# The first key projection moved into the norm of a two-block network kernel, beside the gates and the first query

## The reference

```python
def first_block(x, c, ada_w, ada_b, norm_g, gdn_w_in, ...):
    cond = jax.nn.silu(c)
    mod = cond @ ada_w[i] + ada_b[i]
    shift, scale, gate = jnp.split(mod, 3, axis=-1)
    hdn = rms_norm(x, norm_g[i]) * (1.0 + scale) + shift
    y = gated_deltanet(hdn, ...)
...
def gated_deltanet(h, w_in, conv_w, a_log, dt_bias, norm_w, w_out):
    proj = h @ w_in
    qkv, z, b_lin, a_lin = jnp.split(proj, ...)
    qkv = jax.nn.silu(causal_depthwise_conv(qkv, conv_w))
    q = l2norm(q) * (dh ** -0.5);  k = l2norm(k)
    beta = jax.nn.sigmoid(b_lin)
    g = -jnp.exp(a_log) * jax.nn.softplus(a_lin + dt_bias)
    gc = jnp.cumsum(g, axis=-1)                     # within a chunk
    decay = jnp.exp(gc[..., :, None] - gc[..., None, :])
    ...                                             # chunk by chunk, with a state per head
    return (rms_norm(o, norm_w) * silu(z)) @ w_out
```

## Time and profile before

| | |
|---|---|
| median of 3 runs | 2103.11 us (2101.9 to 2104.24) |
| the profiled execution | 2103.15 us, its span in the trace 2101.4 us |
| PE, DVE, ACT, POOL busy | 95%, 61%, 41%, 7% of the span |
| granted TensorE clock, mean | 0.985 |
| the norm, 30 to 70 us | PE busy 30.30, DVE 36.04 of 40 us, clock 0.79 |
| 150 to 200 us | PE busy 45.45 of 50 us |

### The profile page before, as it was taken

One profiled execution on the slowest core, in us unless ns is written; L12 is line 12 of the kernel. 1 busy time (PEld: TensorE's weight loads), 2 busy tenths in 40 slices (PEclk: granted clock), 3 DMA queues, 4 the chain that ended last, 5 costly groups with the idle time before them and its releaser, 6 DMA issues.

```text
span 2101.4 us, 29428 instructions
## 1 busy us (share of the span) xinstructions
PE 1992.7 (95%) x11256; PEld 1618.2 (77%) x11256; DVE 1272.9 (61%) x2415; ACT 853.5 (41%) x1376; POOL 138.4 (7%) x114
## 2 busy tenths in 40 slices
PE   4989999999999999969998999999999899999998
PEld 2667878888887878857776787777777678888877
DVE  6777777797869686749635644445353435633543
ACT  5644353544345443159403333544443337600321
POOL 0030202021111212000000000000000000000000
PEclk8999999999999999989999999999999999999999
DMA  7222233232323242548213211120312125211232
GB/s 282 86 75 70 87 89 106 65 101 71 105 68 105 67 120 68 168 158 287 80 41 136 66 60 41 41 101 21 111 41 81 61 72 219 91 49 41 85 116 80
DMA packets 128971, 200.27 MB, mean 95 GB/s; under 512 B 56596, under 2 KB 88084, under 8 KB 127808
## 3 DMA queue, kind: packets, MB, share of 16 engines
q1 hardware_dynamic: 128832, 198.39, 29.6%
HBM read 156.22 MB, written 42.11 MB: 94 GB/s over the span
## 4 chain that ended last, share of the span: by engine, by line
PE 47%; DVE 4%; DMA 2%; issue 2%; ACT 1%; SPq 0%; DVEq 0%; ACTq 0%
PE m_job L1682 6%; PE m_job L1684 6%; PE m_job L1683 6%; PE e_b L2369 4%; PE e_b L2371 4%; PE e_b L2370 4%; PE p_out L1352 2%; PE p_out L1353 2%; PE p_out L1354 2%; PE p_sc L1928 2%; PE p_s L1951 2%; PE e_b L2440 1%; PE e_b L2438 1%; PE e_b L2439 1%; DMA m_raw<-in_w 1%
## 5 line engine op out<-in xcount | busy, mean ns | idle before, releaser
L795 PE MATMUL p_job<-h_hi,w_hi 128*128 128x512 f32 x768 | 322.0, 419 | 18.8 <-DVE h_lo L185 17.3
L797 PE MATMUL p_job<-h_hi,w_lo 128*128 128x512 f32 x768 | 302.9, 394 | 0.0
L796 PE MATMUL p_job<-h_lo,w_hi 128*128 128x512 f32 x768 | 302.3, 394 | 0.0
L1682 PE MATMUL m_job<-h_hi,m_hi 128*128 128x512 f32 x576 | 237.6, 413 | 5.3 <-issue 4.2
L1684 PE MATMUL m_job<-h_hi,m_lo 128*128 128x512 f32 x576 | 227.4, 395 | 0.0
L1683 PE MATMUL m_job<-h_lo,m_hi 128*128 128x512 f32 x576 | 226.4, 393 | 0.0
L795 PEld LDWEIGHTS p_job<-h_hi,w_hi 128*128 128x128 f32 x768 | 146.0, 190 | 59.5 <-issue 16.2
L796 PEld LDWEIGHTS p_job<-h_lo,w_hi 128*128 128x128 f32 x768 | 146.1, 190 | 35.4 <-issue 7.9
L797 PEld LDWEIGHTS p_job<-h_hi,w_lo 128*128 128x128 f32 x768 | 145.8, 190 | 31.4
L1682 PEld LDWEIGHTS m_job<-h_hi,m_hi 128*128 128x128 f32 x576 | 108.8, 189 | 52.5 <-issue 31.0
L633 ACT ACTIVATE pre<-p_job 128x512 f32<-128x512 f32 x96 | 56.7, 591 | 179.1 <-PE p_job L797 179.1
(11 more groups left out here) (395 smaller groups left out, 4166.3 us busy)
## 6 DMA issues: line engine op xcount, KB each, us to landing
w_raw<-in_w SPq DMA_DIRECT2D x49, 512.0 KB
m_raw<-in_w SPq DMA_DIRECT2D x49, 512.0 KB, 3.8
rows<-grows SPq DMA_DIRECT2D x32, 512.0 KB, 6.6
ada<-in_ada_w SPq DMA_DIRECT2D x8, 1024.0 KB, 5.3
z_scr<-pre SPq DMA_DIRECT2D x16, 512.0 KB, 2.6
o_scr<-oT SPq DMA_DIRECT2D x64, 128.0 KB, 1.8
ob<-o_scr SPq DMA_DIRECT2D x16, 512.0 KB, 4.8
zb<-z_scr SPq DMA_DIRECT2D x16, 512.0 KB, 4.8
```

Source lines behind the costliest of these rows:

```text
L795: nc.tensor.matmul(bank, hi, h_hi[:, k, cut], start=(k == 0), stop=False)
L796: nc.tensor.matmul(bank, hi, h_lo[:, k, cut], start=False, stop=False)
L797: last = nc.tensor.matmul(bank, lo, h_hi[:, k, cut], start=False, stop=(k == KD - 1))
L1682: nc.tensor.matmul(bank, hi, h_hi[:, k, cut], start=(k == 0), stop=False)
```

## The change

The gates get weights of their own, 48 columns wide (`wg_raw`, `wg_hi`, `wg_lo`), and job 0 reads these. Jobs 1 (query) and 2 (key) now both run in the norm: the query beside the gates in every step, and the key, two slices a step, in the last four. For that the key's weights are loaded behind the fifth modulation tile, cast by ACT behind the fourth high part, and subtracted by POOL. The key's two halves use the banks `p_turn` and `p_pre`, so `gcols` and the first `nsum` wait until ACT has evacuated them. `split(3)`, which was `split(2)`, stands behind the norm on DVE and waits for the query's last matmul. In the list of iteration 0 three jobs stand ahead of `gcols` (the first two are done by then, as `job(i, j) > 2` says), and fewer pieces stand between the masks.

```diff
@@ stage_norm
                 if k == 1:
                     first_weights(1)
+                elif k == RING + 1:
+                    first_weights(2)
             constants()
-            next_weights()
...
                 nc.scalar.activation(h_hi[:, k, :], h[:, k % 3, :], ACT.Copy).then_inc(hi_done, 1)
+                if k == RING:
+                    third_weights()
@@ plan
     if i == 0:
-        send(2 * 2 * KD)
+        send(3 * 2 * KD)
         out.extend([("gcols",), ("bcast", 0)])
-        send(14)
+        send(8)
         out.append(("edge", 0))
         for b in range(4):
             for what in ("decay", "dexp"):
                 out.append((what, 0, b))
-                send(2)
+                send(1)
@@ stage_deltanet: banks, loads, POOL, ACT
-            return (p_mone, p_mtwo)[h] if J == 1 else p_job[h]
+            if J in (1, 2):
+                return (p_mone, p_mtwo)[h] if J == 1 else (p_turn, p_pre)[h][:]
+            return p_job[h]
...
-                    sp.dma_start(w_raw[:], io["w1"][J]).then_inc(w_in, 16)
+                    dst, src = (w_raw[:], io["w1"][J - 1]) if J else (wg_raw[:], io["wg1"])
+                    sp.dma_start(dst, src).then_inc(w_in, 16)
...
+                pool.wait_ge(w_hi_done, 3)
+                nc.gpsimd.tensor_tensor(w_lo[:, 0, :], w_raw[:], w_hi[:, 0, :].bitcast(F32), ALU.subtract
+                                        ).then_inc(w_lo_done, 1)
                 pool.wait_ge(cst, 48)
...
+                    if J == 0:
+                        nc.scalar.activation(pre[0:GATES, 0, TAPS - 1 + h * HALF:TAPS - 1 + (h + 1) * HALF],
+                                             p_job[h][0:GATES, :], ACT.Copy).then_inc(evac_done, 1)
+                        return
...
+                def third_weights():
+                    act.wait_ge(w_in, 48)
+                    nc.scalar.activation(w_hi[:, 0, :], w_raw[:], ACT.Copy).then_inc(w_hi_done, 1)
@@ PE
+                def gate_piece(h, k):
+                    if h == 0 and k == 0:
+                        pe.wait_ge(w_lo_done, 1)
+                    cut = slice(h * HALF, (h + 1) * HALF)
+                    bank = p_job[h][0:GATES, :]
+                    nc.tensor.matmul(bank, wg_hi[:, k, :], h_hi[:, k, cut], start=(k == 0), stop=False)
+                    nc.tensor.matmul(bank, wg_hi[:, k, :], h_lo[:, k, cut], start=False, stop=False)
+                    last = nc.tensor.matmul(bank, wg_lo[:, k, :], h_hi[:, k, cut], start=False, stop=(k == KD - 1))
+                    if k == KD - 1:
+                        last.then_inc(half_done, 1)
+
                 def first_pieces(k):
-                    for J in range(2):
-                        for h in range(2):
-                            piece(J, h, k)
+                    for h in range(2):
+                        gate_piece(h, k)
+                    for h in range(2):
+                        piece(1, h, k)
+                    if k >= KD // 2:
+                        for q in range(2):
+                            for h in range(2):
+                                piece(2, h, 2 * k - KD + q)
...
                         elif s[0] == "gcols":
                             pe.wait_ge(g_dve, 11)
                             pe.wait_ge(g_act, 5)
+                            pe.wait_ge(evac_done, 5)
...
                             if m >= 1:
                                 pe.wait_ge(nln, m)
+                            else:
+                                pe.wait_ge(evac_done, 6)
@@ DVE
                     dve.wait_ge(w_in, 16 * (J + 1))
-                    if J >= 2:
+                    if J >= 3:
                         dve.wait_ge(half_done, 2 * (J - 1))
...
-                split(2)
+                split(3)
@@ kernel
-    nc = bacc.Bacc("TRN2", target_bir_lowering=False, num_devices=1)
+    nc = bacc.Bacc("TRN2", target_bir_lowering=False, num_devices=1, dynamic_dma_scratch_size=1024)
```

More of the change, by code:

```diff
@@ L35 @@
 EPS = 1e-6
+GATES = 48
 QK_HEADS = 8
@@ L104, in stage_norm, with sync @@
         lo_done = sem("a_lo_done")
-        def sync(sp, first_weights, next_weights, constants):
+        def sync(sp, first_weights, constants):
             sp.dma_start(cond[:], io["c"].broadcast_to([P, D])).then_inc(cond_in, 16)
@@ L371, in stage_deltanet @@
         w_raw, w_hi, w_lo, tri, conv_w, adt = (keep[n] for n in ("w_raw", "w_hi", "w_lo", "tri", "conv_w", "adt"))
+        wg_raw, wg_hi, wg_lo = keep["wg_raw"], keep["wg_hi"], keep["wg_lo"]
         pre = sb("pre", [P, 2, TAPS - 1 + T])
@@ L502, in constants @@
                         sp.dma_start(dst, src).then_inc(cst, 16)
-                norm["sync"](sp, load, lambda: load(2), constants)
+                norm["sync"](sp, load, constants)
                 for i in range(N_IT):
@@ L632, in evac @@
                     act.wait_ge(half_done, 2 * J + h + 1)
+                    if J == 0:
+                        nc.scalar.activation(pre[0:GATES, 0, TAPS - 1 + h * HALF:TAPS - 1 + (h + 1) * HALF],
+                                             p_job[h][0:GATES, :], ACT.Copy).then_inc(evac_done, 1)
+                        return
                     nc.scalar.activation(pre[:, J % 2, TAPS - 1 + h * HALF:TAPS - 1 + (h + 1) * HALF], job_bank(J, h)[:],
                                          func).then_inc(evac_done, 1)
-                norm["scalar"](act)
+                def third_weights():
+                    act.wait_ge(w_in, 48)
+                    nc.scalar.activation(w_hi[:, 0, :], w_raw[:], ACT.Copy).then_inc(w_hi_done, 1)
+                norm["scalar"](act, third_weights)
                 def first_tap(i, j):
@@ L787, in piece @@
                         pe.wait_ge(w_lo_done, J + 1)
-                    if k == 0 and J >= 2:
-                        pe.wait_ge(evac_done, 2 * (J - 1) + h + 1 if J > 2 else h + 1)
+                    if k == 0 and J > 3:
+                        pe.wait_ge(evac_done, 2 * (J - 1) + h + 1)
+                    elif k == 0 and J == 3:
+                        pe.wait_ge(evac_done, h + 1)
                     cut = slice(h * HALF, (h + 1) * HALF)
@@ L810, in _ @@
                         if s[0] == "slice":
-                            if job(i, s[1]) > 1:
+                            if job(i, s[1]) > 2:
                                 piece(job(i, s[1]), s[2], s[3])
@@ L939, in split @@
                     dve.wait_ge(w_in, 16 * (J + 1))
-                    if J >= 2:
+                    if J >= 3:
                         dve.wait_ge(half_done, 2 * (J - 1))
-                    nc.vector.tensor_copy(w_hi[:, J % 2, :], w_raw[:]).then_inc(w_hi_done, 1)
+                    raw, hi, lo = (w_raw[:], w_hi[:, J % 2, :], w_lo[:, J % 2, :]) if J else (wg_raw[:], wg_hi[:], wg_lo[:])
+                    nc.vector.tensor_copy(hi, raw).then_inc(w_hi_done, 1)
                     dve.wait_ge(w_hi_done, J + 1)
-                    nc.vector.tensor_tensor(w_lo[:, J % 2, :], w_raw[:], w_hi[:, J % 2, :].bitcast(F32),
-                                            ALU.subtract).then_inc(w_lo_done, 1)
+                    nc.vector.tensor_tensor(lo, raw, hi.bitcast(F32), ALU.subtract).then_inc(w_lo_done, 1)
                 norm["vector"](dve, split)
@@ L986, in _ @@
                     for s in plans[i]:
-                        if s[0] == "split" and 2 < job(i, s[1]) + 1 < N_JOBS:
+                        if s[0] == "split" and 3 < job(i, s[1]) + 1 < N_JOBS:
                             split(job(i, s[1]) + 1)
@@ L2667, in _layout @@
     qk, vw = QK_HEADS * DH, V_HEADS * DH
-    first = [[(0, 2 * qk + 2 * vw, 16), (32, 2 * qk + 2 * vw + 16, 16)]]
-    conv = []
+    gates = [[(0, 2 * qk + 2 * vw, 16), (32, 2 * qk + 2 * vw + 16, 16)]]
+    first, conv = [], []
     for g in range(QK_HEADS + 1):
@@ L2697, in _layout @@
         "w1": _tiles(a["gdn_w_in"][0], first),
+        "wg1": _tiles(a["gdn_w_in"][0], gates, GATES)[0].reshape(P, KD, GATES),
         "conv_w": np.stack([np.stack([cw[:, c:c + P].transpose() for c in own], axis=1) for own in conv], axis=1),
@@ L2735, in build @@
             for name, shape, dt in (("w_raw", [P, KD * P], F32), ("w_hi", [P, 2, KD * P], F32R),
-                                    ("w_lo", [P, 2, KD * P], F32R), ("tri", [P, P], F32),
+                                    ("w_lo", [P, 2, KD * P], F32R), ("wg_raw", [P, KD, GATES], F32),
+                                    ("wg_hi", [P, KD, GATES], F32R), ("wg_lo", [P, KD, GATES], F32R), ("tri", [P, P], F32),
                                     ("conv_w", [P, QK_HEADS, 4, TAPS], F32), ("adt", [P, 3], F32)):
```

2 lines of the change are left out of this document (1 added, 1 removed).

## The result

The changed kernel takes 2110.69 us (median of 11 runs, 2106.68 to 2113.57) where the kernel before took 2103.11 (11 runs, 2097.69 to 2106.33). The ratio is 1.0034 with an interval of 1.0024 to 1.0044, so 0.0034 x 2103 = **7.1 us slower** (5.0 to 9.3). The forecast was 3.5 us slower, 2106.7 in a range of 2101 to 2111: inside the range, near its upper end, with half of the size. The profiled execution is the median one, 2110.69 us.

A forecast was written before the change was run, and what follows sets the result against it. DVE paces the norm, and a chain of DVE steps and transfers shares the timing until the merge. The key's 4.8 us gain is lost in a wait, gram product and merge come 3.5 later: 2103.15 + 3.5 = 2106.7 us, range 2101 to 2111.

The forecast's parts named there:

- The mechanism: Norm to head sum: key 4.8 us earlier on PE, gates 4.4 later, PE's 8 us wait for ACT's square undoing the gain.
- The rival in which PE decides and the gain stays: Whole kernel: the key's 4.8 us on PE are the path, time 2098.3; chance 0.10.
- that of no effect: Whole kernel: late key weights make the norm slip, or unnoticed slack covers the delay; time about 2103; chance 0.12.
- first product of the norm (smaller split; start): Start of the norm: narrower gate weights shorten DVE's first split, but ACT's rinv leaves only 0.3 us of gain.
- DVE beside POOL's subtraction: Norm: DVE loses 2.2 us beside POOL's 2.54 us subtraction, between 1.8 and 2.54.
- head sum to end of the value job, over 9.2 undisturbed: PE behind its 8 us wait: 9.2 us plus 1.4 for the lower clock, value job ending at 99.2.
- first mask difference: DVE, behind split(5), three taps and the key's first half: first decay at 109.0, where it stood at 95.91.
- from there to the key's second product: Four decay blocks pass POOL one by one, 3.47 us each; the key's second norm on DVE reaches 120.0 instead of 116.84.
- key's second product to gram product: Fourth decay adds 0.75 us there, the cast beside POOL saves 0.5; gram product 3.5 us later than 121.36.
- the clock price behind PE's wait: PE behind the 8 us wait at the head sum: one price of 1.4 us, ends 0 and twice that.
- One block of the masks: One decay block on POOL takes 3.47 us, with mask operations put at 1.27 us.
- The rival of the half level in the norm: PE gets the half clock once or twice between 54.9 and 77.0, 1.4 us each; 2109.4; chance 0.16.

The follow-up runs named there:

- run 9: Changed kernel with the query's two head sums behind 15 and 19 pieces instead of 5 and 11 (key's behind 24 and 29); 2.9 us over the kernel before.
- run 7: Changed kernel with ACT's two evacuations of the key and its first tap ahead of the gate exponential; 5.7 us over the kernel before.
- run 11: Changed kernel with 32 matmuls that nothing reads filling PE's wait at the query's first head sum; 3.6 us over the kernel before.
- run 1: Changed kernel with POOL subtracting 8 columns instead of 1024 and PE reading the high part in the low part's place; 5.5 us over the kernel before.
- run 3: Changed kernel with the key's 16 pieces dealt out so that the gates no longer stand behind the key's queue; 5.3 us over the kernel before.
- run 6: Changed kernel with the key's low part subtracted by DVE and multiplied behind the norm, split(3) behind the gate step; 3.6 us over the kernel before.
- run 12: Changed kernel with split(3) behind the gate step on DVE instead of ahead of it; 8.6 us over the kernel before.
- run 5: The kernel before with nothing but the smaller scratch for DMAs; 0.6 us over the kernel before (-1.1 to 2.5).

## Why the prediction was right, and where it was too small

**The mechanism held step by step.** PE runs without a pause from the fifth step to 77.62 (77 forecast), the gates end at 73.54 (72.9), the gate step stands at 77.04 (76.3), the scans end at 86.64 (86.0), the head sum is released by ACT's square at 89.39 (88.6) after a wait of 8.21 us (8). The traces of runs 9 and 7 show that this wait, and ACT's queue that sets it, do take the key's gain back: the gram product comes 6.2 and 2.8 us earlier with gates as late as in the change. The rival in which PE decides and the gain stays (2098.3) is out, and so is that of no effect: the loss is 5.0 to 9.3 us.

**The sizes.** At the first gram product 3.5 us were forecast, and 6.46 measured in the two profiled executions. By the steps:

| step | forecast | measured |
|---|---|---|
| first product of the norm (smaller split; start) | -0.3 | +0.54 |
| DVE beside POOL's subtraction | 2.2 | 2.15 |
| head sum to end of the value job, over 9.2 undisturbed | 1.4 | 3.07 |
| first mask difference | 109.0 | 111.49 |
| from there to the key's second product | 11.0 | 12.02 |
| key's second product to gram product | 4.86 | 4.31 |

*The step that failed is the clock price behind PE's wait.* The forecast took one price of 1.4 us from a stretch of the norm that was granted 0.65 in 4.9 us, behind a wait of 1.79, and kept twice that as an end. Even from that row the price was read too low: 1.4 is the difference of the busy times of 12 and of 14 matmuls, and 12 matmuls at 0.23 are 2.76 us, so the row gives 4.61 - 2.76 = 1.85. Behind 8.21 us the clock was 0.50 for the whole 6.14 us, and cost 101.43 + 0.23 - 89.39 - 9.2 = 3.07. Run 11 shows it as a cause up to the gram product: 2.9 us in the trace, with a time 3.5 us lower. A row from a partly slowed stretch was not the nearest row to a stretch that begins at the lower level.

The price isn't a constant either. From the head sum to the gate columns, over run 11's 9.46 us, it was 2.9 us in the change, 1.5 in run 1 behind the same wait of 8.21 us, and 2.1 to 2.7 in runs 3, 6, 7 and 12 behind waits of 5.59 to 7.37. So one execution near the forecast's 1.4 exists; that the profiled one had the highest of the six is in part chance.

*The start of the norm* was 0.84 us later than forecast. ACT's rinv was done at 25.62 instead of 24.77, because the first loads landed later. Over the twelve traces of changed kernels, with the same loads ahead of it, it lies between 23.79 and 25.67, and in the two of before at 24.77 and 24.13, so nothing ties it to the change.

*One block of the masks* was 1.0 us longer: POOL's first triangle took 2.34 us beside DVE's differences, which the forecast had put at 1.27.

*The 2.2 us on DVE were right for a wrong reason.* They were chosen between 1.8 (0.71 per POOL time) and 2.54 us (the whole of POOL's operation, as two adds). In the trace POOL's instruction starts at 46.12 beside DVE's product, which ends undisturbed at 47.29, and POOL's ends at 49.49; DVE's sum of one column, issued at 47.21, ends at 49.51. If POOL stood still until 47.29, as its 8 columns in run 1 suggest (recorded 1.22 us beside a product of 1.22), its own time is 2.20 us, and DVE lost nearly all of it, 2.15. The Trainium skill, page "SBUF — State Buffer", section "SBUF: two separate sides", says that whichever of the two has the shared port pair keeps it for the whole instruction; trace and run 1 agree, down to an instruction of 0.15 us that waits for 2.15.

**Behind the gram product** the loss shrank from 6.46 to 5.18 us at the second group's rows, where the forecast let it stand; 1.0 of that goes with the lower clock behind the merge in the trace of before, which was that of an execution with a long first stage (run 5). Against the mean of both traces of before, the change's first stage is 263.55 - 256.95 = 6.6 us longer, close to the 7.1 measured.

**The rival of the half level in the norm** (2109.4) named the right cause, a lower clock, in the wrong place: in the norm the change ran at 1.00 from the fifth step on.

## What to carry to other kernels

Work that is moved into a neighbour's idle time delays whatever shares its queues: here the key gained 4 us on PE and the gates, which everything behind hangs on, lost 5. Look for the instruction that the moved work's result still waits behind, on every engine (ACT's gate exponential here), and move that too, or the gain ends in a wait; and price a wait of PE by the clock it resumes at, not by its length alone, and as a range: waits of the same 8.21 us cost 1.5 us in one trace and 2.9 in another. One profiled execution is not the kernel: take a second one of the same program before trusting a difference of 4 us in 260.

## What was not expected of the hardware

The same program's first stage (the scratch apart) took 258.91 us in one execution and 254.99 in another, and the stretches at the lower clock level fell on other steps: the norm's last step was granted 0.74 or 1.00, the 5.6 us behind the merge 0.50 or 0.70. The gate step and the stretch from the merge to the second group's rows hold 2.7 of the 3.9 us (1.6 and 1.1). The Trainium skill, page "TensorE: Matmul & The Clock Gate", section "Part 1: The HAM clock gate", says that the throttled state is the default, that activity releases it, and that the number of slow matmuls differs from run to run; these two traces agree.

Matmuls that nothing reads made the changed kernel faster by about 3.5 us in the median (run 11; 1.5 to 5.5 over before instead of 5.0 to 9.3, so the size is loose); in its trace the real ones behind them ran at 1.00 instead of 0.50.

A DVE instruction on one column, 0.15 us elsewhere, was recorded with 2.30 us beside POOL's subtraction, and POOL's subtraction of 8 columns with 1.22 us beside a DVE product: the trace puts the wait into the instruction's own duration, and no idle time shows.
